# Interleaving the sums of the first SSM output projections, and projecting the gates two pairs ahead

## The reference

```python
def gated_group_rms_norm(y, z, w, groups):
    g = y * jax.nn.silu(z.astype(jnp.float32))
    shp = g.shape
    gg = g.reshape(shp[:-1] + (groups, shp[-1] // groups))
    gg = gg * lax.rsqrt(jnp.mean(gg * gg, axis=-1, keepdims=True) + RMS_EPS)
    return gg.reshape(shp) * w
...
    y = ssd_chunked(xs * dt[..., None], a, b_in, c_out)
    y = y + d_skip.astype(jnp.float32)[:, None] * xs
    y = gated_group_rms_norm(y.reshape(bsz, seq, SSM_D_INNER), z, norm_w, SSM_N_GROUPS)
    return y.astype(u.dtype) @ out_w
```

## Time and profile before

| | |
|---|---|
| median of three runs | 964.98 us |
| profiled execution | 967.93 us |
| its span | 966.1 us |
| TensorE busy | 891.1 us (92%) |
| VectorE busy | 586.1 us (61%) |
| ScalarE busy | 483.3 us (50%) |
| GpSimd busy | 620.0 us (64%) |
| pairs loop, from the start of `sz0` to that of `so0` | 113.3 to 204.0 us |

### The profile page before, as it was taken

One profiled execution on the slowest core, in us unless ns is written; L12 is line 12 of the kernel. 1 busy time (PEld: TensorE's weight loads), 2 busy tenths in 40 slices (PEclk: granted clock), 3 DMA queues, 4 the chain that ended last, 5 costly groups with the idle time before them and its releaser, 6 DMA issues.

```text
span 966.1 us, 18261 instructions
## 1 busy us (share of the span) xinstructions
PE 891.1 (92%) x7019; PEld 852.7 (88%) x7019; DVE 586.1 (61%) x1582; ACT 483.3 (50%) x920; POOL 620.0 (64%) x274
## 2 busy tenths in 40 slices
PE   7999899989998899999998995978989999999995
PEld 7999888879997799999988984857879999999995
DVE  6986567762255544443479867676666666751155
ACT  6754465534544365555535364444445454454451
POOL 3899645537885356548777794222366888878970
PEclk9999999998999999999999898889999999999998
DMA  8577432223654243445555564121245666666621
GB/s 323 178 218 216 136 110 88 89 66 109 193 179 131 73 125 110 134 129 153 175 155 155 168 204 127 49 84 47 85 131 153 197 190 192 181 187 179 200 84 44
DMA packets 38534, 138.85 MB, mean 144 GB/s; under 512 B 4272, under 2 KB 4272, under 8 KB 38448
## 3 DMA queue, kind: packets, MB, share of 16 engines
q1 hardware_dynamic: 38448, 137.69, 46.9%
HBM read 136.63 MB, written 1.05 MB: 142 GB/s over the span
## 4 chain that ended last, share of the span: by engine, by line
PE 65%; DVE 16%; issue 3%; ACT 3%; POOL 1%; DVEq 0%; ACTq 0%
PE ps L538 17%; PE ps L540 17%; PE ps L539 17%; DVE ps L1379 2%; DVE ps L1525 2%; DVE nnm L1673 1%; PE ps L733 1%; DVE root L1383 1%; PE ps L571 1%; PE ps L735 1%; PE ps L545 1%; POOL wl L499 1%; PE ps L547 1%; PE ps L546 1%; PE ps L563 1%
## 5 line engine op out<-in xcount | busy, mean ns | idle before, releaser
L499 POOL TENSOR_TENSOR wl<-raw,wh 128x1024 fp32r<-128x1024 f32 x254 | 608.5, 2417 | 297.5 <-ACT wh L970 297.5
L538 PE MATMUL ps<-uh,wh 128*128 128x256 f32 x1248 | 357.3, 286 | 5.3 <-DVE ul L1460 2.2
L539 PE MATMUL ps<-ul,wh 128*128 128x256 f32 x1248 | 352.1, 282 | 0.0
L540 PE MATMUL ps<-uh,wl 128*128 128x256 f32 x1248 | 351.8, 282 | 0.0
L970 ACT ACTIVATE wh<-raw 128x1024 fp32r<-128x1024 f32 x256 | 263.1, 1054 | 124.7 <-PE ps L540 121.5
L538 PEld LDWEIGHTS ps<-uh,wh 128*128 128x128 f32 x1248 | 238.7, 191 | 11.1 <-issue 4.1
L539 PEld LDWEIGHTS ps<-ul,wh 128*128 128x128 f32 x1248 | 238.8, 191 | 0.0
L540 PEld LDWEIGHTS ps<-uh,wl 128*128 128x128 f32 x1248 | 238.5, 191 | 0.0
L1618 DVE TENSOR_TENSOR h<-ps,h 128x256 f32<-128x256 f32 x32 | 13.6, 425 | 118.4 <-PE ps L540 118.3
L538 PE MATMUL ps<-ffh,wh 128*128 128x256 f32 x176 | 49.1, 279 | 0.0
L539 PE MATMUL ps<-ffl,wh 128*128 128x256 f32 x176 | 49.1, 279 | 0.0
(11 more groups left out here) (355 smaller groups left out, 1835.0 us busy)
## 6 DMA issues: line engine op xcount, KB each, us to landing
raw<-slabs SPq DMA_DIRECT2D x256, 512.0 KB, 3.7
h<-x_fm SPq DMA_DIRECT2D x4, 256.0 KB, 5.3
out_fm<-outb SPq DMA_DIRECT2D x4, 256.0 KB, 2.2
cst<-shape_consts SPq DMA_DIRECT2D x1, 768.0 KB, 7.8
vec<-vectors SPq DMA_DIRECT2D x1, 303.5 KB, 4.0
pin<-p_fm SPq DMA_DIRECT2D x1, 256.0 KB, 4.1
```

Source lines behind the costliest of these rows:

```text
L499: nc.gpsimd.tensor_tensor(wl[:, s % PART_RING, :], raw[:, s % RAW_RING, :], wh[:, s % PART_RING, :].bitcast(f32), ALU.subtract).then_inc(s ...
L538: nc.tensor.matmul(res, w_h, a_h, start=first, stop=False)
L539: nc.tensor.matmul(res, w_h, a_l, start=False, stop=False)
L540: ins = nc.tensor.matmul(res, w_l, a_h, start=False, stop=last)
```

## The change

Five things change together. (1) TensorE issues `sz0` and `sz1` ahead of the transposes, scores and decays of pair 0, and in iteration j of the loop `sz(j+2)` in place of `sz(j+1)`. (2) The loop has a sixteenth iteration; in iterations 14 and 15 the first 8 steps of `so0` and `so1` stand where a gate's projection stood. The heads 30 and 31 come at the end of iteration 15 as all others do. (3) The remaining steps of `so0`, `so1` and `so2` are issued in parts (8 to 12, 12 to 14, 14 to 16), each part for all three, with the last norms between them; their three sums stand in three banks at the same time. (4) The weights of these three outputs are laid into the stream in that order, and ScalarE waits for a new count (`slab_done`) where a slab ends with an unfinished sum. The number of slabs is the same. (5) The last norm, of four tiles, becomes two of two tiles. ScalarE's feeding and GpSimd's low parts move by one slab. VectorE's list is the same except behind pair 15.

```diff
+SO_FIRST = 3
+SPLIT = {"so0": [(f"so{n}", 0, 8) for n in range(SO_FIRST)] + [(f"so{n}", 8, 12) for n in range(SO_FIRST)]
+         + [(f"so{n}", 12, 14) for n in range(SO_FIRST)] + [(f"so{n}", 14, 16) for n in range(SO_FIRST)]}
+
 
 
 def plan():
     jobs, block, out = {}, 0, 0
     used = {"act": 0, "dve": 0}
     freed = []
-    done_with = {}
+    parts = []
     for name, array, cols, _, kind, consumer in weight_jobs():
         kt, wide = K_OF[array], len(cols) // P
-        if wide > 1 and block % wide:
-            block += wide - block % wide
-        j = jobs[name] = Job(name, kind, kt, wide, block, out, consumer, used[consumer])
+        j = jobs[name] = Job(name, kind, kt, wide, out, consumer, used[consumer])
         for _ in range(j.n_out):
             used[consumer] += 1
             freed.append((consumer, used[consumer]))
-        block += j.blocks
         out += j.n_out
-        for s in range(j.slab0, j.slab1 + 1):
-            done_with[s] = out
-    return jobs, freed, done_with, -(-block // BLK)
+        if name in SPLIT:
+            parts += SPLIT[name]
+        elif not any(name == n for split in SPLIT.values() for n, _, _ in split):
+            parts.append((name, 0, kt))
+    last_use = {}
+    for name, k0, k1 in parts:
+        j = jobs[name]
+        block += -block % j.wide
+        for k in range(k0, k1):
+            j.at[k] = block
+            last_use[block // BLK] = (name, k)
+            block += j.wide
+    done_with, releases = {}, {}
+    for s, (name, k) in sorted(last_use.items()):
+        j = jobs[name]
+        if k == j.kt - 1:
+            done_with[s] = ("proj_done", j.out + j.n_out)
+        else:
+            releases[name, k] = len(releases) + 1
+            done_with[s] = ("slab_done", releases[name, k])
+    return jobs, freed, done_with, releases, -(-block // BLK)
...
-        for g in range(SSM_G - 1):
-            last = g == SSM_G - 2
-            n_grp.append(Norm((lambda k, g=g: gb[:, (2 * g + k) % 4, :]), 4 if last else 2, 256, ("ssm_nw", 2 * g),
+        for g in range(SSM_G):
+            n_grp.append(Norm((lambda k, g=g: gb[:, (2 * g + k) % 4, :]), 2, 256, ("ssm_nw", 2 * g),
                               (lambda k, g=g: ("gated", 2 * g + k + 1)),
                               (lambda k, g=g: ynh[:, 2 * g + k, :]), (lambda k, g=g: ynl[:, 2 * g + k, :]),
-                              sqb=(lambda k, g=g: sq[:, (2 * g + k) % 8, :]), groups=2 if last else 1,
+                              sqb=(lambda k, g=g: sq[:, (2 * g + k) % 8, :]),
                               pool_low=True))
...
-                    if s == jobs["sz0"].slab0 + min(2 * g + 10, 2 * SSM_G + 5):
+                    if s == jobs["sz0"].slab0 + min(2 * g + 11, 2 * SSM_G + 6):
...
+                project_part(name, hi, lo, 0, jobs[name].kt, ready)
+
+            def project_part(name, hi, lo, k0, k1, ready=None):
+
                 j = jobs[name]
                 for o in range(j.out, j.out + j.n_out):
-                    if o >= PROJ_BANKS:
+                    if o >= PROJ_BANKS and k0 == 0:
                         who, n = freed[o - PROJ_BANKS]
                         wait(pe, f"{who}_evac", n)
...
-                for k in range(j.kt):
+                for k in range(k0, k1):
                     if ready:
                         ready(k)
-                    b = j.block + k * j.wide
+                    b = j.at[k]
...
+                    if (name, k) in releases:
+                        ins.then_inc(sem("slab_done"), 1)
...
+            def so_part(n, k0, k1):
+
+                project_part(f"so{n}", tile_of(ynh), tile_of(ynl), k0, k1,
+                             lambda k: wait(pe, "norm_lo", n_grp[0].p0 + k + 1))
+
+            project("sz0", u, u_lo)
+            project("sz1", u, u_lo)
             wait(pe, "decay_parts", 1)
             x_transpose(0)
             cb_scores(0)
             decay(0)
             decay(1)
-            project("sz0", u, u_lo)
-            for j in range(SSM_PAIRS - 1):
-                project(f"sz{j + 1}", u, u_lo)
-                if j % 2:
-                    cb_scores((j + 1) // 2)
-                x_transpose(j + 1)
-                decay(2 * j + 2)
-                decay(2 * j + 3)
+            for j in range(SSM_PAIRS):
+                if j + 2 < SSM_PAIRS:
+                    project(f"sz{j + 2}", u, u_lo)
+                else:
+                    so_part(j + 2 - SSM_PAIRS, 0, 8)
+                if j + 1 < SSM_PAIRS:
+                    if j % 2:
+                        cb_scores((j + 1) // 2)
+                    x_transpose(j + 1)
+                    decay(2 * j + 2)
+                    decay(2 * j + 3)
                 if j % 2 and j >= 3:
 
-                    wait(pe, "cb_evac", (j + 3) // 2)
+                    wait(pe, "cb_evac", min((j + 3) // 2, SSM_G))
                     norm_sum(n_grp[(j - 3) // 2])
                 if j % 2 == 0 and j >= 4:
                     norm_spread(n_grp[(j - 4) // 2])
                 head_out(2 * j)
                 head_out(2 * j + 1)
-
-            def last_groups(k):
-
-                if k == 5:
-                    head_out(2 * SSM_PAIRS - 2)
-                    head_out(2 * SSM_PAIRS - 1)
-                elif k == 8:
-                    norm_sum(n_grp[6])
-                elif k == 12:
-                    norm_spread(n_grp[6])
-                wait(pe, "norm_lo", n_grp[0].p0 + k + 1)
-
-            for n in range(KD):
-                project(f"so{n}", tile_of(ynh), tile_of(ynl), last_groups if n == 0 else None)
+            so_part(2, 0, 8)
+            norm_spread(n_grp[6])
+            so_part(0, 8, 12)
+            so_part(1, 8, 12)
+            norm_sum(n_grp[7])
+            so_part(2, 8, 12)
+            for n in range(SO_FIRST):
+                so_part(n, 12, 14)
+            norm_spread(n_grp[7])
+            for n in range(SO_FIRST):
+                so_part(n, 14, 16)
+            for n in range(SO_FIRST, KD):
+                project(f"so{n}", tile_of(ynh), tile_of(ynl))
...
-                        act.wait_ge(sem("proj_done"), done_with[s - PART_RING])
+                        act.wait_ge(sem(done_with[s - PART_RING][0]), done_with[s - PART_RING][1])
...
-                n = n_grp[min(t // 2, SSM_G - 2)]
+                n = n_grp[t // 2]
...
-                if j + 1 < SSM_PAIRS:
-                    feed(f"sz{j + 1}")
+                feed(f"sz{j + 2}" if j + 2 < SSM_PAIRS else f"so{j + 2 - SSM_PAIRS}")
...
-            feed("so0")
             square_group(SSM_PAIRS - 1)
             high_parts(n_grp[6])
+            high_parts(n_grp[7])
             feed_and_square("so", n_mla)
...
-                if j % 2 and 3 <= j < SSM_PAIRS - 1:
+                if j % 2 and j >= 3:
                     inverse_root(n_grp[(j - 3) // 2])
-            norm(n_grp[6])
+            norm_tiles(n_grp[6])
+            norm(n_grp[7])
```

More of the change, by code:

```diff
@@ L173, with __init__ @@
 class Job:
-    def __init__(self, name, kind, kt, wide, block, out, consumer, used):
-        self.name, self.kind, self.kt, self.wide, self.block, self.out = name, kind, kt, wide, block, out
+    def __init__(self, name, kind, kt, wide, out, consumer, used):
+        self.name, self.kind, self.kt, self.wide, self.out = name, kind, kt, wide, out
         self.consumer, self.used = consumer, used
@@ L180, in __init__, with slab0 @@
         self.blocks = kt * wide
-        self.slab0, self.slab1 = block // BLK, (block + self.blocks - 1) // BLK
+        self.at = [None] * kt
+    @property
+    def slab0(self):
+        return self.at[0] // BLK
+SO_FIRST = 3
+SPLIT = {"so0": [(f"so{n}", 0, 8) for n in range(SO_FIRST)] + [(f"so{n}", 8, 12) for n in range(SO_FIRST)]
+         + [(f"so{n}", 12, 14) for n in range(SO_FIRST)] + [(f"so{n}", 14, 16) for n in range(SO_FIRST)]}
 def plan():
@@ L224, in build @@
     ALU, ACT, AX = mybir.AluOpType, mybir.ActivationFunctionType, mybir.AxisListType
-    jobs, freed, done_with, n_slabs = plan()
+    jobs, freed, done_with, releases, n_slabs = plan()
     VC, n_vec = vector_columns()
@@ L2025, in pack_weights @@
 def pack_weights(inputs):
-    jobs, _, _, n_slabs = plan()
+    jobs, _, _, _, n_slabs = plan()
     stream = np.zeros((n_slabs * BLK, P, P), np.float32)
@@ L2037, in pack_weights @@
         blocks = w.reshape(j.kt, P, j.wide, P).transpose(0, 2, 1, 3).reshape(j.blocks, P, P)
-        stream[j.block:j.block + j.blocks] = blocks
+        for k in range(j.kt):
+            stream[j.at[k]:j.at[k] + j.wide] = blocks[k * j.wide:(k + 1) * j.wide]
     return np.ascontiguousarray(stream.reshape(n_slabs, BLK, P, P).transpose(0, 2, 1, 3).reshape(n_slabs, P, SLAB))
```

## The result

The changed kernel takes 970.13 us in the median of 8 executions (967.16 to 974.55), the kernel before 965.03 us (963.90 to 966.74, 8 executions). The ratio is 1.0050 with a 95% interval of 1.0028 to 1.0073: 5.1 us slower. 967.7 us had been forecast, with a range of 963.5 to 972.0 and 0.72 for slower; the narrower range of the forecast alone, without its rivals, was 966.2 to 969.2, and the measured median lies above it. The execution that was profiled is the longest of the eight, 974.55 us with a span of 972.8 us; so the profile is read for where time goes, and not for the sum.

A forecast was written before the change was run, and what follows sets the result against it. TensorE, busy 891 of 966 us, was taken to bound the kernel. Terms -5.2 + 13.2 - 6.1 + 0.8 = +2.7 us on the 964.98 us median gave 967.7 us, range 963.5 to 972.0.

The forecast's parts named there:

- rival (a): One or two clock drops, at iteration 1's projection or behind the last spreading: 1.5 or 3 us more, 969.2 to 970.7; chance 0.25.
- start of the loop: At the start of the pairs loop, two early projections cover TensorE's 3.71 us wait for the decay banks: 5.2 us gained.
- the loop: In the pairs loop, a new wait for szb at 15 projections, about 0.9 us each: 13.2 us lost.
- behind the loop: After the pairs loop, output projections in parts cover most waiting for the last norms: 6.1 us gained.
- second slab of `so3`: Feeding of this weight slab stands behind so0's square and rounding on ScalarE, so TensorE waits: 0.8 us lost.
- The ring: In the loop, sz(j+2) needs szb(j-1)'s bank, closing a cycle through TensorE, ScalarE and VectorE: iterations of 6.76 and 6.82 us.
- The signal: In the loop, time from the end of szb to the next projection's start: 0.1 us, bounds 0 and 0.2.
- The first wait: TensorE's wait for szb ahead of iteration 1's projection, with one slab fed in 1.05 us: 1.4 us.
- Rival (d): An overlooked wait, in ScalarE's list around iteration 15 or GpSimd's around the last low parts: 1 to 3 us more; chance 0.08.
- The clock: TensorE's granted clock takes no drop, its longest waits being 1.4 us in the loop and 1.85 behind the last spreading.
- Rival (c): In the loop, szb comes earlier since VectorE scales the gate sooner: 961.8 us, chance 0.12; bank never holding TensorE: 954.5, 0.03.
- Rival (b): The clock swings in the loop, every second iteration losing 1.5 us: 10.5 us more, 978 us; chance 0.04.

The follow-up runs named there:

- gate_in_sbuf: The changed kernel, but VectorE scales each gate out of PSUM into an SBUF tile, freeing its bank before szb: 956.52 us, ratio 0.9923.
- szb_first: The changed kernel with szb moved ahead of both mb in VectorE's list: 957.97 us, ratio 0.9933.
- ring_in_before: The kernel before with one added wait: the projection of gate j+1 (from gate 2 on) waits for szb of pair j-1: 978.41 us, ratio 1.0132.
- feed_one: The changed kernel, but ScalarE feeds one weight slab in place of two in iteration 0: 968.05 us, ratio 1.0043.
- spread_early: The changed kernel, but the last norm's spreading comes ahead of the part 12 to 14 of so2: 968.91 us, ratio 1.0052.
- after_again: The changed kernel itself run once more, nothing altered, beside the kernel before on another chip: 969.96 us, ratio 1.0047.
- one_ahead_parts: The changed kernel with the gates one pair ahead, as before, and the outputs still in parts: 960.83 us, ratio 0.9962.

## Why the prediction was right, step by step

The sign and the mechanism were right; the time was 2.4 us low, for reasons that have names. It came out above the forecast's own range and inside the wider one, at the place where rival (a) stood. The stages in the profiles, with the steps of the prediction:

| step | forecast | measured in the profiles | how |
|---|---|---|---|
| start of the loop | -5.2 | -5.4 | 119.63 + 0.51 - 114.76 |
| the loop | +13.2 | +15.3 | (217.29 - 114.76) - (204.03 - 119.63) - 2.80 |
| behind the loop | -6.1 | -4.8 | (240.20 - 217.29 + 2.80) - (234.52 - 204.03) |
| second slab of `so3` | +0.8 | +0.4 | 246.18 - 240.20 - 5.60 |
| sum | +2.7 | +5.5 | |

With the 0.51 us that this profile was late at the start these 5.5 are 6.1 us at the fourth output; the other 0.6 us of the spans' difference lie later, and medians differ by 5.1. In particular:

- **The ring** was right in place, partners and size. 15 waits, from the fourth on 0.47 and 1.42 us in turn (0.5 and 1.4 had been read off the rows of before), iterations of 6.71 and 6.83 us (6.76 and 6.82). gate_in_sbuf took it away, szb_first shortened it, ring_in_before made it without the change, each within about 2 us of what the theory gave. The signal, put at 0.1 us, took 0.05. It stands nine times in the sum, so its bounds of 0 and 0.2 us give 12.3 and 14.1, and not 12.4 and 14.0.
- **The first wait was mis-sized**: 2.32 and not 1.4 us. The step that failed is the feeding in iteration 0, put at one slab, 1.05 us. `feed("sz0")` before the loop is followed by `feed("sz2")` in iteration 0, so two slabs are due there: 2.02 us on ScalarE, ahead of the tanh and both exponentials of the ring. feed_one shows the wait at 1.36 us with one slab. Rival (d) had an overlooked wait in ScalarE's list, but at the other end of the loop.
- **The clock.** The prediction kept it at 1.00, since in the profile of before it was at 0.50 behind a wait of 2.34 us and at 1.00 behind one of 2.04, and its own longest wait was 1.85 us. That reading of two rows was no rule (last section). Behind the real first wait of 2.3 us it was at 0.50 in all three profiles whose list has that wait (changed kernel, its repetition, spread_early), and iteration 1 took 8.06 us (the next projection starts at 129.90), where 6.76 had been forecast: 1.3 us. Feeding and clock make 0.9 + 1.3 = 2.2 us, the whole miss of the loop's term.
- **Behind the loop** the waits were right: 1.12 us for the root (1.2), 1.82 for the low part (1.83). `so1` and `so2` ended 1.28 us apart and not 0.7, at half clock. That is rival (a), which had a chance of 0.25: both of its drops came, the first of them behind a wait longer than (a) had assumed. Without the two (1.3 us and 2 x 0.58 us) the sum of the stages would be about 3.0 us, near the forecast: nearly half of the loss in this profile is the clock's, and the sum had it at nothing.
- **The second slab of `so3`**: TensorE waited 0.6 us for `wl` in six of the other kernels (0.8 forecast); in the changed kernel it fell to under half a microsecond. This fits `so0` having been complete longer before `so3` began, as the sums of `so1` and `so2` ran at half clock: in the six kernels with the wait the clock was at 1.00 there.
- **Rival (c)** was wrong: VectorE scales the gate earlier, but then waits for TensorE's transposes (2.76 us) and for the exponentials (0.75 us, the row at 181.83) all the same, and no time reaches `szb`.
- **Rival (b)** was wrong: 89 us with a wait in each iteration at a granted clock of 1.00. The Trainium skill, "TensorE: Matmul & The Clock Gate", section "A second HAM failure mode: psum-queue depth-cycling", tells of such a swing in another kernel and gives no length of the short idling. This trace does not show it, with waits of 0.5 to 1.4 us every 6.8 us.

## What to carry to other kernels

Before an operation is moved ahead, count the buffers: with three banks in turn, running one step further ahead turns the release of the last one into a wait, and if that release depends on the waiting engine's own earlier work it is a ring that is paid in every iteration. Its price can be read from the profile before, as the distance from where TensorE would start to where the reader of the bank ends, followed once around. The cure is at the release and not at the projection: scaling the gate out of the bank (12 us by the ratios to before, 13 by the medians of two chips) or moving its last reader up in the list (12 us) kept what the early projections were worth.

## What the runs showed of the clock

The length of a wait does not settle alone whether the clock falls. The next mixer (MLA) has two waits that all ten profiles share. These rows are from the two profiles of the changed kernel, one program, first `after` and then `after_again`:

```profile
300.75 0.47 PE L573 MATMUL ps<-wh,ckh 128*128 128x512 f32 x1 [2.34 <-issue]
301.00:305.00 4.00, 3.96 (x17) 2.93 (x17) 3.86 (x6) 2.87 (x5) 2.62 (x1) 1.00 0.09 30
326.10 1.11 PE L747 MATMUL ps<-rx,cst 128*128 128x256 f32 x2 [2.03 <-DVE r L1685]
327.00:329.00 2.00, 2.00 (x11) 1.99 (x10) 1.71 (x2) 0.38 (x1) 2.00 (x1) 0.50 0.32 131
...
301.13 0.47 PE L573 MATMUL ps<-wh,ckh 128*128 128x512 f32 x1 [2.34 <-issue]
302.50:305.00 2.50, 2.50 (x8) 1.86 (x7) 2.49 (x2) 0.60 (x1) 2.46 (x1) 0.50 0.00 0
327.76 0.67 PE L747 MATMUL ps<-rx,cst 128*128 128x256 f32 x2 [2.04 <-DVE r L1685]
328.00:331.00 3.00, 2.18 (x17) 1.92 (x16) 2.86 (x4) 0.94 (x3) 2.60 (x1) 1.00 0.36 145
```

One execution kept the clock behind 2.34 us and lost it behind 2.03, the other the reverse. Over the ten profiles of this case the clock fell to 0.50 behind the wait of 2.34 us in eight, and behind that of 2.04 us in seven. The pair of rows in the profile of before from which the prediction took its clock was one draw of this.

In the loop it fell behind the first wait of 2.3 us in all three profiles that have it; behind the loop's other waits, up to 1.5 us, never. Behind the last wait of 1.82 us, with the same instructions around it, it fell in both profiles of the changed kernel (0.50 from about a microsecond after TensorE's restart) and not in feed_one, gate_in_sbuf, one_ahead_parts and szb_first (1.00). What decides between 1.8 and 2.3 us is open. So a wait of this length is best forecast with and without a drop, each with a chance; one profile cannot tell which.

The changed kernel's executions spread over 7 to 8 us, the four of gate_in_sbuf over 1.3 us, but the ten of one_ahead_parts spread over 8.7 us and those of the kernel before, in the second group, over 10.5 us. That the drops make this spread was not shown.
